# Token mean squares at a mixer's end: fifteen column products instead of row sums and transposes

## The chip, the cores and the metric

The kernel runs on one core of a Trainium2 chip. The metric is the device time of one launch in microseconds (us). The engines are TensorE (PE; its weight loads are listed apart as PEld), VectorE (DVE), ScalarE (ACT), GpSimd (POOL) and SyncE (SP), which issues most of the transfers. Each engine runs its own list of instructions in order and waits for others on semaphores.

## What is computed

A decoder trunk of two layers. Each layer adds half of a normed SwiGLU network to x, then a mixer, then half of a second SwiGLU network. All is in float32. The part that the change touches is the end of the mixer, which in the reference reads:

```python
lru_out = rmsnorm((hl * jax.nn.gelu(yl.astype(jnp.float32))).astype(h.dtype), p['lru_norm'])   # over 512 channels
...
o = rmsnorm(o, p['gla_norm']).reshape(B, T, D_GLA)                 # per head, over 128 channels, 4 heads
gla_out = (o * jax.nn.silu(g.astype(jnp.float32))).astype(h.dtype)
out = jnp.concatenate([lru_out, gla_out], axis=-1) @ p['w_out']
```

So each token needs five mean squares: one over the recurrence's 512 channels and one for each of four attention heads over its 128 channels. Each is turned into 1/sqrt(mean + eps) and multiplies that token's values.

## The kernel before

**Tiling.** The tokens are split into two groups of 288 (256 of the prompt and 32 sampled ones); channels lie on the 128 partitions, tokens along the row. There are two layers and two groups, so four mixers, numbered 0 to 3 here (mixer 1 is layer 0, group 1). A "unit" is one output tile of 128 channels: `unit` (line 446) forms it with three matmuls per input tile (the weight and the operand are each split in a high and a low part), 24 matmuls of 128x288 for a depth of 8. TensorE runs 656 units one after the other; results land in three banks of PSUM (`psD`) in turn. For each unit ScalarE makes the high part of the weight (`wh`, line 757), VectorE the low part (`wl`, line 1051, an operation with both inputs in SBUF), and VectorE or ScalarE takes the result out of its bank.

**Sides.** All else is written as generators, "sides", which each engine advances by one slot after every unit: `sides.step()`. What sets the order of the work around the change are therefore slot numbers. A mixer's attention starts after the 20 units of its input projection, and while it goes on, units of the other group's feed-forward network run. In these networks an even slot of the stretch spoken of here follows a gate unit and an odd slot an up unit. After an up unit VectorE forms `hid`, ScalarE its high part `hidh`, and GpSimd its low part `hidl` (line 1698), which waits for `hidh`. GpSimd's `sides.step()` for an odd slot comes right behind that `hidl`.

**The mixer's end.** With `T_SUMS = 31`:

- slot 2: ScalarE squares the recurrence's result into `squares` (128 x 4 x 288), long before it is needed. Slot 30: ScalarE squares the attention's result into `vT` (a part of the tile `qkv`), 4 x 288 wide, one tile per head.
- slot 31: TensorE adds the squares over the partitions with a stationary operand `pick` of 128x5, which is a column of 1/512 or 1/128 and zeros elsewhere: four matmuls of `squares` (line 687) and four of `vT` (line 690) accumulate in `psS` as 5 rows of 288. Each float32 matmul is two records in the trace. ScalarE adds eps and copies them to `rows` (line 950), with GpSimd forming the first half of `gT * oT` (line 1663) meanwhile.
- slot 32: TensorE transposes `rows` in three pieces (line 695), so that the tokens lie on 96 partitions, as 96x15. ScalarE copies that to `cols`; GpSimd's `root` raises it to -1/2 (`inv`, line 1483) and splits it in a high and a low part (`split`, lines 1491 and 1493).
- slots 34, 35 and 36: VectorE multiplies each of the five sets of 3 columns onto an identity, `diag` (line 1065, both inputs in SBUF, 96x576, two buffers), two, two and one of them; at the end of the same slots TensorE turns each into a row that is spread over all partitions (`spread`, lines 484 and 485), into `psS` for the recurrence and the four banks of `psM` for the heads. In slot 33 GpSimd forms the second half of `gT * oT` (line 1665).
- from slot 36 (`T_VALUES`): VectorE multiplies the eight tiles, ScalarE and GpSimd split them, and from unit 44 or 46 on the output projection uses them.

`columns` (line 452) is there already: for the norms between the sub-layers it takes 96 tokens' squares as the stationary operand (128x96) and a column `means` (128x1) as the moving one, so that a mean over the partitions comes out as a column of 96 partitions.

Of the kernel before, what the change touches and what calls it, by code (L numbers as in the profile page):

```python
# [12 lines left out]
P = 128  # L13
# [56 lines left out]
T_VALUES = T_SUMS + 5  # L70
# [93 lines left out]
def program(nc, a, ctx):  # L164
# [49 lines left out]
    means = sb("means", [P, 1])  # L214
    pick = sb("pick", [P, STATS, STATS])
# [40 lines left out]
    squares, val, eb, qe, gd, rows = [], [], [], [], [], []  # L256
    for g in range(G):
# [9 lines left out]
        rows.append(sb(f"rows{g}", [STATS, T]))  # L267
# [23 lines left out]
    rows_ready, rows_kept = sem("rows_ready"), sem("rows_kept")  # L291
# [135 lines left out]
    def _(e):  # L427
# [22 lines left out]
        def columns(src, first, stop):  # L450
            for t in range(NTC):
                mm = e.matmul(psS[0:TC, 0, 288 + t:289 + t], src[:, t * TC:(t + 1) * TC], means[:, :],  # L452
                              start=(first and t == 0), stop=stop, skip_group_check=True)
            return mm
# [215 lines left out]
        def attention(s):  # L670
            i, g = s.mixer, s.g
            for slot in range(T_VALUES + 2):
# [10 lines left out]
                if slot == T_SUMS:  # L683
                    sums_free()
                    e.wait_ge(lru_squared, i + 1)
                    for t in range(LT):
                        e.matmul(psS[0:STATS, 0, 0:T], pick[:, 0, :], squares[g][:, t, :], start=(t == 0), stop=False)  # L687
                    e.wait_ge(head_squared, i + 1)
                    for h in range(HEADS):
                        mm = e.matmul(psS[0:STATS, 0, 0:T], pick[:, 1 + h, :], vT[:, h, :], start=False, stop=(h == HEADS - 1))  # L690
                    mm.then_inc(rows_ready, 1)
                if slot == T_SUMS + 1:
                    e.wait_ge(rows_kept, i + 1)
                    for t in range(NTC):
                        mm = e.transpose(psS[0:TC, 0, 288 + t * STATS:288 + (t + 1) * STATS], rows[g][:, t * TC:(t + 1) * TC],
                                         ident[0:STATS, 0:STATS])
                    mm.then_inc(cols_ready, 1)
                    event[0] += 1
                    last_use.append((val_ready, 8 * i + LT))
                if slot == T_SUMS + 4:  # L700
                    spread_one()
                    e.wait_ge(s_ready, 3 * i + 3)
                for h in range(HEADS):
                    if slot == T_SUMS + 4 + (h + 1) // 2:
                        spread(psM[:, h, 0:T])
# [39 lines left out]
    def _(e):  # L745
# [182 lines left out]
        def attention(s):  # L928
            i, g = s.mixer, s.g
            for slot in range(T_VALUES + DT // 2):  # L930
# [15 lines left out]
                if slot == T_SUMS:  # L946
                    e.wait_ge(rows_ready, i + 1)
                    if i:
                        e.wait_ge(cols_kept, event[0])
                    e.activation(rows[g][:, :], psS[0:STATS, 0, 0:T], ACT.Identity, bias=epsc[0:STATS, :]).then_inc(rows_kept, 1)  # L950
                if slot == T_SUMS + 1:
                    keep_sums(STATS * NTC, True)
# [83 lines left out]
    def _(e):  # L1036
# [41 lines left out]
        def stat_diagonal(k):  # L1078
            diagonal(split[:, :, :].bitcast(F32).rearrange("p s (t k) -> p s t k", k=STATS)[:, :, :, k])
# [195 lines left out]
        def attention(s):  # L1275
            i, g = s.mixer, s.g
            for slot in range(T_VALUES + DT // 2):
# [31 lines left out]
                if slot == T_SUMS + 3:  # L1309
# [4 lines left out]
                if slot == T_SUMS + 4:  # L1314
                    stat_diagonal(2)
                    stat_diagonal(3)
                if slot == T_SUMS + 5:
# [139 lines left out]
    def _(e):  # L1457
# [184 lines left out]
        def attention(s):  # L1642
            i, g = s.mixer, s.g
            for slot in range(T_VALUES + DT // 2 + 1):
# [3 lines left out]
                for c, at in enumerate(T_QUERIES):  # L1648
# [24 lines left out]
        e.memset(means[:, :], 1.0 / D)  # L1673
        for k in range(STATS):
            e.memset(pick[:, k, k:k + 1], 1.0 / (DV if k else DL))
            if k < STATS - 1:
                e.memset(pick[:, k:k + 2, :].rearrange("p a b -> p (a b)")[:, k + 1:k + 1 + STATS], 0.0)
# [121 lines left out]
```

## Time and profile before

| what | us |
|---|---|
| median of 3 runs | 2247.0 (2244.05 to 2248.79) |
| the profiled execution, its own time | 2245.68 |
| its span in the trace | 2243.9 |
| TensorE busy | 2223.9 (99%) |
| VectorE / ScalarE / GpSimd busy | 1359.2 / 1179.7 / 734.7 |

Lines are those of the kernel before. A matmul's own duration in the rows includes its latency, and matmuls overlap: what a stretch costs TensorE is read from the distance between starts. Within a unit of the main product starts lie 0.133 us apart (24 of them take 3.2 us).

### The profile page before, as it was taken

To read this page: it belongs to the slowest core of one execution; us is meant where nothing else is said; L and a number is where in the kernel's file an instruction comes from. 1 tells how busy PE (TensorE), PEld (TensorE's weight loads), DVE (VectorE), ACT (ScalarE), POOL (GpSimd) and SP (SyncE) were. 2 spreads that over 40 slices of the span, in tenths; PEclk is the share of its full clock that TensorE was granted. 3 is DMA by queue.
4 is the path that set the end of the run, shared out by engine and by line. 5 is a ranking of instruction groups with operands and counts; after the bars stand their busy time and mean duration, and the time that the engine had idled before them with its cause. 6 is when DMAs were issued, how large, how long until landed. Compare 5 with 4: busy or idle time off the path is not lost.

```text
span 2243.9 us, 40461 instructions
## 1 busy us (share of the span) xinstructions
PE 2223.9 (99%) x16890; PEld 2187.1 (97%) x16890; DVE 1359.2 (61%) x1771; ACT 1179.7 (53%) x1840; POOL 734.7 (33%) x793
## 2 busy tenths in 40 slices
PE   9999999999999999999999999999999999999998
PEld 8999999999999999999999999999999999999998
DVE  6554757647785466755574547576578755475454
ACT  6544557536675345544454355574367653464433
POOL 4012413416544224521241124134264523252112
PEclk9999999999999999999999999999999999999999
DMA  6555555445544355555555555554354443555553
GB/s 228 161 164 165 161 169 159 132 120 163 160 147 136 117 173 155 169 160 167 162 163 165 162 167 161 167 158 129 123 176 151 142 133 122 180 161 160 166 163 129
DMA packets 102261, 350.62 MB, mean 156 GB/s; under 512 B 11296, under 2 KB 16416, under 8 KB 102080
## 3 DMA queue, kind: packets, MB, share of 16 engines
q1 hardware_dynamic: 100848, 346.76, 50.6%
q8 instruction: 135, 2.21, 0.4%
q10 hardware_dynamic: 1232, 1.27, 0.2%
q14 instruction: 46, 0.38, 0.0%
HBM read 343.12 MB, written 4.87 MB: 155 GB/s over the span
## 4 chain that ended last, share of the span: by engine, by line
PE 93%; DVE 3%; POOL 2%; issue 2%; ACT 0%; DMA 0%; SPq 0%; DVEq 0%; POOLq 0%
PE psD L446 87%; DVE wl L1051 1%; POOL ssum L1470 1%; PE psM L588 1%; DVE hl L1103 1%; PE psM L564 1%; PE psM L648 1%; PE psM L637 0%; PE psS L452 0%; DVE y L1089 0%; PE psM L666 0%; DVE x L1093 0%; PE psS L687 0%; PE psS L690 0%; DMA x<-in_xT 0%
## 5 line engine op out<-in xcount | busy, mean ns | idle before, releaser
L446 PE MATMUL psD<-hh,wh 128*128 128x288 f32 x3712 | 1111.5, 299 | 4.1 <-issue 1.3
L446 PE MATMUL psD<-hl,wh 128*128 128x288 f32 x3712 | 1098.7, 296 | 0.0
L446 PE MATMUL psD<-hh,wl 128*128 128x288 f32 x3712 | 1094.9, 295 | 0.0
L1051 DVE TENSOR_TENSOR wl<-raw,wh 128x1024 fp32r<-128x1024 f32 (+1 forms) x656 | 818.0, 1247 | 133.5 <-ACT wh L757 133.4
L757 ACT ACTIVATE wh<-raw 128x1024 fp32r<-128x1024 f32 (+1 forms) x656 | 672.4, 1027 | 106.3 <-DMA raw<-in_w_gu 52.1
L446 PEld LDWEIGHTS psD<-hh,wh 128*128 128x128 f32 x3712 | 699.3, 188 | 13.0 <-issue 8.3
L446 PEld LDWEIGHTS psD<-hh,wl 128*128 128x128 f32 x3712 | 702.5, 189 | 0.0
L446 PEld LDWEIGHTS psD<-hl,wh 128*128 128x128 f32 x3712 | 700.7, 189 | 1.0
L1698 POOL TENSOR_TENSOR hidl<-hid,hidh 128x288 fp32r<-128x288 f32 x176 | 210.0, 1193 | 941.1 <-ACT hidh L1001 941.1
L446 PE MATMUL psD<-hidh,wh 128*128 128x288 f32 x1408 | 417.5, 297 | 0.0
L446 PE MATMUL psD<-hidl,wh 128*128 128x288 f32 x1408 | 415.5, 295 | 0.0
L446 PE MATMUL psD<-hidh,wl 128*128 128x288 f32 x1408 | 415.1, 295 | 0.0
L446 PEld LDWEIGHTS psD<-hidh,wh 128*128 128x128 f32 x1408 | 264.0, 187 | 2.4 <-issue 0.7
L446 PEld LDWEIGHTS psD<-hidh,wl 128*128 128x128 f32 x1408 | 264.9, 188 | 0.0
L446 PEld LDWEIGHTS psD<-hidl,wh 128*128 128x128 f32 x1408 | 264.4, 188 | 0.0
L1470 POOL TENSOR_TENSOR ssum<-ssum,sq 128x288 f32<-128x288 f32 x166 | 193.6, 1169 | 176.7 <-ACT sq L769 173.2
L1001 ACT ACTIVATE hidh<-hid 128x288 fp32r<-128x288 f32 x176 | 78.2, 445 | 328.2 <-DVE hid L1057 328.0
L1057 DVE TENSOR_TENSOR hid<-psD,act 128x288 f32<-128x288 f32 x176 | 80.4, 457 | 258.8 <-PE psD L446 258.3
L997 ACT ACTIVATE act<-gate 128x288 f32<-128x288 f32 x176 | 78.4, 445 | 284.5 <-DVE gate L1057 283.8
L1057 DVE TENSOR_TENSOR gate<-psD,rstd 128x288 f32<-128x288 f32 x176 | 80.2, 456 | 226.8 <-PE psD L446 226.4
L1418 DVE TENSOR_TENSOR y<-psD,y 128x288 f32<-128x288 f32 x128 | 58.5, 457 | 141.0 <-PE psD L446 140.9
L1008 ACT ACTIVATE y<-psD 128x288 f32<-128x288 f32 x64 | 26.4, 413 | 119.4 <-PE psD L446 119.4
(191 smaller groups left out, 1516.2 us busy)
## 6 DMA issues: line engine op xcount, KB each, us to landing
raw<-in_w_gu SPq DMA_DIRECT2D x352, 512.0 KB, 3.6
raw<-in_w_d SPq DMA_DIRECT2D x128, 448.0 KB, 3.2
raw<-in_w_in SPq DMA_DIRECT2D x80, 512.0 KB, 3.6
raw<-in_w_d SPq DMA_DIRECT2D x64, 512.0 KB, 3.6
raw<-in_w_out SPq DMA_DIRECT2D x32, 512.0 KB, 3.6
gates<-in_w_ax SPq DMA_DIRECT2D x4, 512.0 KB, 4.7
S<-in_st_gla SPq DMA_DIRECT2D x4, 512.0 KB, 4.5
out_gla_s<-S SPq DMA_DIRECT2D x4, 512.0 KB, 5.4
```

What stands on the lines that cost most here:

```text
L446: mm = e.matmul(out, w[:, kt * P:(kt + 1) * P], t[:, kt, :], start=(kt == 0 and part == 0), stop=(kt == KT - 1 and part == 2))
L564: mm = e.matmul(psM[:, gate_of, 0:T], gates[:, t, gate_of * P:(gate_of + 1) * P], xc[g][:, :], start=True, stop=True)
L588: mm = e.matmul(psM[0:n, 2 + odd, pr * 256 + v * (n // 2):pr * 256 + (v + 1) * (n // 2)], K[rows, pr, v, 0:n], q, start=(pr == 0 and v == ...
L757: e.activation(wh[u % RING][:, 0:width], raw[u % RING][:, 0:width], ACT.Copy).then_inc(hi_ready, 1)
L997: e.activation(act[:, :], gate[:, :], ACT.Silu).then_inc(silu_ready, 1)
L1001: e.activation(hidh[:, j, :], hid[:, :], ACT.Copy).then_inc(hidh_ready, 1)
L1008: e.activation(y[g][:, m, :], bank(u), ACT.Copy).then_inc(out_taken_act, 1)
L1051: e.tensor_tensor(wl[u % RING][:, 0:width], raw[u % RING][:, 0:width], wh[u % RING][:, 0:width].bitcast(F32), ALU.subtract).then_inc(lo_re ...
L1057: e.tensor_tensor(out, bank(u), by, ALU.mult).then_inc(out_taken, 1)
L1418: e.tensor_tensor(y[g][:, m, :], bank(u), y[g][:, m, :], ALU.add).then_inc(out_taken, 1)
L1470: e.tensor_tensor(ssum[g][:, :], ssum[g][:, :], sq[g][m % 2][:, :], ALU.add).then_inc(sq_used[g], 1)
L1698: e.tensor_tensor(hidl[:, j, :], hid[:, :], hidh[:, j, :].bitcast(F32), ALU.subtract).then_inc(hidl_ready, 1)
```

## The change

The stationary operand `pick`, the tile `rows` and its two semaphores go. `means` has three columns (1/1024, 1/512 and 1/128). In slot 15 of the attention (`T_LRU_SUM`) GpSimd adds the recurrence's four tiles of squares to one, in place, in two steps. In slot 31 TensorE forms `columns` of that sum and of the four heads: 3 + 12 products with a stationary operand of 128x96 and a moving one of 128x1. The result lies in `psS` as before, but grouped by statistic, so that `stat_diagonal` takes three columns in a row. ScalarE's copy to `cols` adds eps, in slot 31, and GpSimd's `root` is in slot 31. The halves of `gT * oT` are in slots 32 and 33. The diagonals, the spreads and the values stand one slot earlier: 33 to 35, and from 35 on.

```diff
-T_VALUES = T_SUMS + 5
+T_LRU_SUM = 15
+T_VALUES = T_SUMS + 4
...
-    means = sb("means", [P, 1])
-    pick = sb("pick", [P, STATS, STATS])
+    means = sb("means", [P, 3])
...
                 if slot == T_SUMS:
                     sums_free()
-                    e.wait_ge(lru_squared, i + 1)
-                    for t in range(LT):
-                        e.matmul(psS[0:STATS, 0, 0:T], pick[:, 0, :], squares[g][:, t, :], start=(t == 0), stop=False)
+                    e.wait_ge(lru_summed, i + 1)
+                    columns(squares[g][:, 0, :], True, True, 1)
                     e.wait_ge(head_squared, i + 1)
                     for h in range(HEADS):
-                        mm = e.matmul(psS[0:STATS, 0, 0:T], pick[:, 1 + h, :], vT[:, h, :], start=False, stop=(h == HEADS - 1))
-                    mm.then_inc(rows_ready, 1)
-                if slot == T_SUMS + 1:
-                    e.wait_ge(rows_kept, i + 1)
-                    for t in range(NTC):
-                        mm = e.transpose(psS[0:TC, 0, 288 + t * STATS:288 + (t + 1) * STATS], rows[g][:, t * TC:(t + 1) * TC],
-                                         ident[0:STATS, 0:STATS])
+                        mm = columns(vT[:, h, :], False, True, 2, (1 + h) * NTC)
                     mm.then_inc(cols_ready, 1)
...
-                if slot == T_SUMS + 4:
+                if slot == T_SUMS + 3:
                     spread_one()
...
                 if slot == T_SUMS:
-                    e.wait_ge(rows_ready, i + 1)
-                    if i:
-                        e.wait_ge(cols_kept, event[0])
-                    e.activation(rows[g][:, :], psS[0:STATS, 0, 0:T], ACT.Identity, bias=epsc[0:STATS, :]).then_inc(rows_kept, 1)
-                if slot == T_SUMS + 1:
-                    keep_sums(STATS * NTC, True)
+                    keep_sums(STATS * NTC)
...
-                if slot == T_SUMS + 3:
+                if slot == T_SUMS + 2:
                     inverse_ready()
                     before = spreads[0]
                     stat_diagonal(0)
                     stat_diagonal(1)
-                if slot == T_SUMS + 4:
+                if slot == T_SUMS + 3:
...
+                if slot == T_LRU_SUM:
+                    e.wait_ge(lru_squared, i + 1)
+                    steps.mark(e.tensor_tensor(squares[g][:, 0:2, :], squares[g][:, 0:2, :], squares[g][:, 2:4, :], ALU.add))
+                    steps.after()
+                    e.tensor_tensor(squares[g][:, 0, :], squares[g][:, 0, :], squares[g][:, 1, :], ALU.add).then_inc(lru_summed, 1)
+                if slot == T_SUMS:
+                    root(STATS * NTC)
                 if slot == T_SUMS + 1:
-                    root(STATS * NTC)
-                if slot == T_SUMS:
                     e.wait_ge(g_ready, i + 1)
```

**TensorE, slot 31 of mixer 0**, between the last matmul of one unit and the first two of the next. Before:

```order
L446 MATMUL psD<-hh_53,wl_76 128x288
L687 MATMUL psS<-squares_150,pick 5x288 x4
L690 MATMUL psS<-qkv,pick 5x288 x4
L446 MATMUL psD<-hh_53,wh_59 128x288
L446 MATMUL psD<-hl_54,wh_59 128x288
```

and changed:

```order
L445 MATMUL psD<-hh_53,wl_76 128x288
L451 MATMUL psS<-means,squares_149 96x1 x3
L451 MATMUL psS<-means,qkv 96x1 x12
L445 MATMUL psD<-hh_53,wh_59 128x288
L445 MATMUL psD<-hl_54,wh_59 128x288
```

Eight float32 matmuls of 288 columns have become fifteen of one column; the three transposes that stood one unit further down are gone.

**GpSimd, slots 23 to 35 of mixer 0** (the row with x5 is the low parts of five up units, the last of them that of slot 31). Before:

```order
L1698 TENSOR_TENSOR hidl<-hid,hidh 128x288 x5
L1663 TENSOR_TENSOR gT<-gT,oT 128x576
L1483 TENSOR_TENSOR inv<-cols,minus_half 96x15
L1491 CAST split<-inv 96x15
L1493 TENSOR_TENSOR split<-inv,split 96x15
L1698 TENSOR_TENSOR hidl<-hid,hidh 128x288
L1665 TENSOR_TENSOR gT<-gT,oT 128x576
L1698 TENSOR_TENSOR hidl<-hid,hidh 128x288
```

and changed (the last three places of the list are the low part of slot 33's unit, the second half of `gT * oT`, and the low part of slot 35's):

```order
L1687 TENSOR_TENSOR hidl<-hid,hidh 128x288 x5
L1470 TENSOR_TENSOR inv<-cols,minus_half 96x15
L1478 CAST split<-inv 96x15
L1480 TENSOR_TENSOR split<-inv,split 96x15
L1655 TENSOR_TENSOR gT<-gT,oT 128x576
L1687 TENSOR_TENSOR hidl<-hid,hidh 128x288
L1657 TENSOR_TENSOR gT<-gT,oT 128x576
L1687 TENSOR_TENSOR hidl<-hid,hidh 128x288
```

The root has moved ahead of the low part of slot 33's unit. The second `gT` is right behind that low part in both, but what VectorE has to do at that time is another thing now, as the next lists show.

**VectorE, slots 33 to 35 of mixer 0** (`hid` and `gate` take a unit's result out of its bank). Before:

```order
L1057 TENSOR_TENSOR hid<-psD,act 128x288
L1051 TENSOR_TENSOR wl_75<-raw_69,wh_63 128x896
L1057 TENSOR_TENSOR gate<-psD,rstd_81 128x288
L1051 TENSOR_TENSOR wl_76<-raw_70,wh_64 128x896
L1065 TENSOR_TENSOR diag_89<-ident,split 96x576
L1065 TENSOR_TENSOR diag_88<-ident,split 96x576
L1057 TENSOR_TENSOR hid<-psD,act 128x288
L1051 TENSOR_TENSOR wl_71<-raw_65,wh_59 128x896
L1065 TENSOR_TENSOR diag_89<-ident,split 96x576
L1065 TENSOR_TENSOR diag_88<-ident,split 96x576
```

and changed:

```order
L1044 TENSOR_TENSOR hid<-psD,act 128x288
L1038 TENSOR_TENSOR wl_75<-raw_69,wh_63 128x896
L1052 TENSOR_TENSOR diag_89<-ident,split 96x576
L1052 TENSOR_TENSOR diag_88<-ident,split 96x576
L1044 TENSOR_TENSOR gate<-psD,rstd_81 128x288
L1038 TENSOR_TENSOR wl_76<-raw_70,wh_64 128x896
L1052 TENSOR_TENSOR diag_89<-ident,split 96x576
L1052 TENSOR_TENSOR diag_88<-ident,split 96x576
L1044 TENSOR_TENSOR hid<-psD,act 128x288
L1038 TENSOR_TENSOR wl_71<-raw_65,wh_59 128x896
```

The first two diagonals stood behind a `gate` (an even slot), in which GpSimd has no low part to form; now they stand behind a `hid` (an odd slot).

## Rows read from the trace of the kernel before

**Rows 1.** The page's first part: busy time, share of span, instructions of each engine.

```profile
PE 2223.9 (99%) x16890; PEld 2187.1 (97%) x16890; DVE 1359.2 (61%) x1771; ACT 1179.7 (53%) x1840; POOL 734.7 (33%) x793
```

**Rows 2.** Timeline of TensorE, mixer 0's sums: start us, us, line, names, count.

```profile
496.75 0.29 PE L446 MATMUL psD<-hh,wl 128*128 128x288 f32 x1
496.97 2.10 PE L687 MATMUL psS<-squares,pick 128*5 128x288 f32 x8
...
501.18 0.30 PE L446 MATMUL psD<-hl,wh 128*128 128x288 f32 x1
...
504.11 0.29 PE L446 MATMUL psD<-hh,wl 128*128 128x288 f32 x1
...
504.81 0.29 PE L446 MATMUL psD<-hl,wh 128*128 128x288 f32 x1
```

**Rows 3.** Timeline of TensorE at two places where column products stand already.

```profile
640.93 0.29 PE L446 MATMUL psD<-hh,wl 128*128 128x288 f32 x1
641.07 0.59 PE L452 MATMUL psS<-means,ssum 128*96 128x1 f32 x6
641.52 0.38 PE L446 MATMUL psD<-hh,wh 128*128 128x288 f32 x1
641.73 0.29 PE L446 MATMUL psD<-hl,wh 128*128 128x288 f32 x1
...
2024.52 0.29 PE L446 MATMUL psD<-hh,wl 128*128 128x288 f32 x1
...
2025.84 0.30 PE L446 MATMUL psD<-hl,wh 128*128 128x288 f32 x1
```

**Rows 4.** Timeline of TensorE around the first two spreads, mixers 0 and 3.

```profile
514.14 0.29 PE L446 MATMUL psD<-hh,wl 128*128 128x288 f32 x1
...
514.90 0.30 PE L446 MATMUL psD<-hidh,wh 128*128 128x288 f32 x1
...
1892.90 0.29 PE L446 MATMUL psD<-hh,wl 128*128 128x288 f32 x1
...
1894.28 0.29 PE L446 MATMUL psD<-hh,wh 128*128 128x288 f32 x1
```

**Rows 5.** Timeline of VectorE at the spreads of mixer 0, then mixer 3.

```profile
513.00 1.41 DVE L1065 TENSOR_TENSOR diag<-ident,split 96x576 fp32r<-96x576 f32 x2
514.57 0.46 DVE L1057 TENSOR_TENSOR hid<-psD,act 128x288 f32<-128x288 f32 x1 [0.16 <-PE psD L446]
514.94 1.08 DVE L1051 TENSOR_TENSOR wl<-raw,wh 128x896 fp32r<-128x896 f32 x1
515.94 2.03 DVE L1065 TENSOR_TENSOR diag<-ident,split 96x576 fp32r<-96x576 f32 x2
...
1890.40 2.05 DVE L1051 TENSOR_TENSOR wl<-raw,wh 128x1024 fp32r<-128x1024 f32 x1
```

**Rows 6.** Timeline of GpSimd at the same two places.

```profile
515.59 1.11 POOL L1698 TENSOR_TENSOR hidl<-hid,hidh 128x288 fp32r<-128x288 f32 x1 [3.46 <-ACT hidh L1001]
...
1889.95 1.43 POOL L1665 TENSOR_TENSOR gT<-gT,oT 128x576 f32<-128x576 f32 x1
```

**Rows 7.** Timelines of GpSimd, VectorE and TensorE in mixer 0's slots 14 to 16.

```profile
428.87 4.54 POOL L1630 TENSOR_TENSOR qf<-dec,qkv 128x768 f32<-128x768 f32 x2
...
431.61 2.75 DVE L1236 TENSOR_TENSOR kf<-dec,qkv 128x896 f32<-128x896 f32 x1
...
436.04 0.38 PE L617 MATMUL psM<-ident,kf 128*128 128x128 f32 x2
```

**Rows 8.** Busy time (count) by stretch: PE, PEld, DVE, ACT, POOL; PEclk, DMA share, GB/s.

```profile
482.00:483.00 1.00, 1.00 (x12) 0.98 (x12) 0.00 (x0) 0.00 (x0) 0.00 (x0) 0.50 0.33 123
486.00:489.00 3.00, 3.00 (x15) 3.00 (x14) 0.00 (x0) 0.00 (x0) 0.00 (x0) 0.54 0.00 0
757.00:762.00 5.00, 5.00 (x22) 5.00 (x23) 0.00 (x0) 0.00 (x0) 0.00 (x0) 0.52 0.00 0
628.00:629.00 1.00, 0.14 (x1) 0.15 (x1) 1.00 (x3) 0.98 (x3) 0.67 (x2) 0.85 0.78 315
```

More of the change, by code:

```diff
@@ L255, in program @@
     xc, rg, ig, tau, aa, l1, l2 = ([], [], [], [], [], [], [])
-    squares, val, eb, qe, gd, rows = [], [], [], [], [], []
+    squares, val, eb, qe, gd = [], [], [], [], []
     for g in range(G):
@@ L266, in program @@
         qe.append(sb(f"qe{g}", [P, PR, C]))
-        rows.append(sb(f"rows{g}", [STATS, T]))
         assert cursor[0] <= result_at[g] + DT * T * 4
@@ L290, in program @@
     setup_v, setup_a, setup_p, wgdh_ready, wgdl_ready = (sem(k) for k in ("setup_v", "setup_a", "setup_p", "wgdh_ready", "wgdl_ready"))
-    rows_ready, rows_kept = sem("rows_ready"), sem("rows_kept")
+    lru_summed = sem("lru_summed")
     sq_ready, sq_used = [sem(f"sq_ready{g}") for g in range(G)], [sem(f"sq_used{g}") for g in range(G)]
@@ L448, in unit, with columns @@
             mm.then_inc(unit_done, 1)
-        def columns(src, first, stop):
+        def columns(src, first, stop, k=0, at=0):
             for t in range(NTC):
-                mm = e.matmul(psS[0:TC, 0, 288 + t:289 + t], src[:, t * TC:(t + 1) * TC], means[:, :],
+                mm = e.matmul(psS[0:TC, 0, 288 + at + t:289 + at + t], src[:, t * TC:(t + 1) * TC], means[:, k:k + 1],
                               start=(first and t == 0), stop=stop, skip_group_check=True)
@@ L703, in attention @@
                 for h in range(HEADS):
-                    if slot == T_SUMS + 4 + (h + 1) // 2:
+                    if slot == T_SUMS + 3 + (h + 1) // 2:
                         spread(psM[:, h, 0:T])
@@ L1078, in stat_diagonal @@
         def stat_diagonal(k):
-            diagonal(split[:, :, :].bitcast(F32).rearrange("p s (t k) -> p s t k", k=STATS)[:, :, :, k])
+            diagonal(split[:, :, k * NTC:(k + 1) * NTC].bitcast(F32))
         def inverse_ready():
@@ L1313, in attention @@
                     stat_diagonal(1)
-                if slot == T_SUMS + 4:
+                if slot == T_SUMS + 3:
                     stat_diagonal(2)
                     stat_diagonal(3)
-                if slot == T_SUMS + 5:
+                if slot == T_SUMS + 4:
                     stat_diagonal(4)
@@ L1672, in _ @@
         e.memset(ones[:, :].bitcast(F32), 1.0)
[L1673 to L1677, printed above, removed]
+        for k, width in enumerate((D, DL, DV)):
+            e.memset(means[:, k:k + 1], 1.0 / width)
         e.memset(qkvs[:, 0:PR], DK ** -0.5)
```

## Prediction

> **What bounds the kernel now.** I read the busy times first, and there is little to choose: TensorE is busy for 2223.9 of 2243.9 us, 99%, the others for 61% or less [rows 1]. A microsecond of work less on TensorE is a microsecond less of time, as long as nobody makes it wait in return; and a wait anywhere else costs nothing until TensorE has it. So the views to read are the timelines of TensorE at the mixers' ends, and then those of the two engines that must have the diagonals ready for it. The reader should look at distances between starts there, not at durations: two neighbouring matmuls of a unit start 0.133 us apart, and whatever stands between them costs the distance less 0.133 us for each ordinary step.
>
> **What goes from TensorE.** In mixer 0 the last matmul of a unit starts at 496.75, the row sums at 496.97, and the second matmul of the next unit at 501.18 [rows 2]. That is 4.43 us with two ordinary steps in it, so the eight float32 matmuls cost 4.43 - 0.27 = 4.16 us. The transposes: from 504.11 to 504.81 [rows 2], 0.70 - 0.27 = 0.43 us. Together 4.59 us a mixer, and the other three mixers have the same distances within 0.02 us.
>
> **What comes to TensorE.** Column products stand in the trace already, with the same 128x96 operand and the same moving column. Three of them (six records) lie between 640.93 and 641.73: 0.80 - 0.27 = 0.53 us. Six, in two groups with a wait between that is long fulfilled, lie between 2024.52 and 2025.84: 1.32 - 0.27 = 1.05 us [rows 3]. So three cost 0.53 us and each further three 0.52, and fifteen cost 0.53 + 4 x 0.52 = 2.61 us. The ends: 2.25 us, if all went like the first three, which take 0.45 us from their first start at 641.07 to 641.52, and 2.65 us, if each three paid the 0.53. The gain is 4.59 - 2.61 = 1.98 us a mixer, 7.9 us in all (7.8 to 9.4).
>
> What these products spend is the load of their stationary operand, a fresh one for each record: 0.52 us for six loads is 87 ns each. The Trainium skill, page "TensorE: Matmul & The Clock Gate", section "LDWEIGHTS (loading the stationary operand)", gives a load as its columns over 1.2, which is an estimate of 80 ns for 96 columns and 2.4 us for the thirty. By that page the gain would be 8.8 us rather than 7.9; the rows of this trace decide, and they say 87.
>
> **The sum of squares on GpSimd** is a 128x576 and a 128x288 operation. The nearest rows are a 128x576 product, 1.43 us, and a low part of 128x288, 1.11 us [rows 6], so 2.5 us a mixer. In slot 15 of mixer 0 it comes behind the two `qf` that end at 433.41, while VectorE's `kf`, started at 431.61, is waiting [rows 7]; `kf` gets its turn first (below) and ends at 434.36 as before, and TensorE needs it only at 436.04, 1.7 us later. Should GpSimd's first addition get ahead of `kf`, it would still be there in time. Everything behind it on GpSimd (the exponents of the third chunk, `qe`) moves by 2.5 us and has several slots. I take nothing; the upper end is the 0.8 us by which both additions together, ahead of `kf`, would overrun the 1.7, in the two mixers of group 0.
>
> **The diagonals** are where I see the gain go. Rows 5 and 6 show a rule of this kernel: a VectorE operation with both inputs in SBUF and a GpSimd operation do not run at the same time, and they take turns. Two diagonals take 1.41 us when GpSimd is idle and 2.03 us when the low part `hidl` (from 515.59) is waiting: `hidl` gets the gap between `wl` and the first diagonal. In mixer 3 `wl`, which for its 1024 columns would take some 1.2 us by the 1.08 for 896, takes 2.05 because the second half of `gT * oT` runs from 1889.95 for 1.43 us [rows 5, 6]. The Trainium skill says the same on its page "SBUF — State Buffer", section "Who interferes with whom": an exclusive lock that is held for a whole instruction, not a split of the bandwidth. By that rule, which these rows bear out, the turns below follow.
>
> Before, the first two diagonals stood behind a gate unit, the next two behind an up unit. Now the first two stand behind the up unit of slot 33, and GpSimd has two operations for that moment, `hidl` and right behind it the second `gT`. I lay the old slot 35 under the new slot 33: its unit's last matmul starts at 514.14 [rows 4], `hid` 514.57, `wl` 514.94 to 516.02, `hidl` waits from 515.59 and ends at 516.70, the first diagonal is done at about 517.33 and the second at 517.97 [rows 5, 6]. With `gT` queued behind `hidl`, `gT` gets the turn after the first diagonal and holds it for 1.3 us, and the second diagonal ends at 519.3. TensorE, one gate unit of 3.2 us further on, arrives at the first spread at 514.14 + 3.2 + 0.13 = 517.47, finds it ready, and at the second at 517.74, where it waits until 519.35: 1.6 us. Then `hid`, `gate` and the later diagonals catch up, since the next pair stands behind a gate unit with an idle GpSimd.
>
> Before, the same pair cost in mixer 0 (514.14 to 514.90, less one step and four spread matmuls of 0.133) 0.10 us of waiting, in mixer 3 (1892.90 to 1894.28) 0.71 [rows 4]; mixers 1 and 2, read alike, 0.36 and 0.10, in all 1.3 us. Now it is 4 x 1.6 = 6.4 us, so 5.1 us more. The fifth diagonal, behind an up unit too, may bring 0.3 us in the mixers of group 0, and the later pair no longer waits 0.3: nothing, in sum. The ends for the diagonals: 0 (the turns fall otherwise) and 7 us.
>
> **TensorE's clock.** The trace shows that the clock falls from 2.4 to 1.2 GHz (granted 1.00 to 0.50) not only when TensorE idles, as between 628 and 629 us, where it is busy for 0.14 us, but also while it is 100% busy with matmuls of few columns: at 482 us of mixer 0, behind the sampled tokens' outputs, it stands at 0.50 [rows 8]. Fifteen products of one column for 2.6 us are such a stretch; the row sums streamed 288 columns each, and the clock stayed up. A fall costs what the full products behind it lose. In 486 to 489 us there are 15 matmuls where 22.5 would start: 1.0 us lost; in 757 to 762, 22 for 37.5: 2.1 us lost [rows 8]. Those stretches behind the outputs are longer (4.9 to 6.8 us) than 2.6, and the column products of before, at most 1.05 us at once, never brought a fall. 2.6 us lies between, so the price is 0 to 2.1 us a mixer, and I take 1.5 us in one or two of the four: 2.2 us. It is nearest to the idle stretch at 628 us.
>
> **The sum.** -7.9 + 5.1 + 2.2 = -0.6 us. The profiled execution took 2245.68 us, its span and 1.8 us around it; the median of the runs is 1.3 us above it, and the sum is small enough to carry over: 2246.4 us.
>
> **The rivals.** (a) The turns fall otherwise and the diagonals come in time. For it speaks that GpSimd's operations could reach their turn earlier than I laid them, or `gT` a little before `hidl`; against it that the two stand side by side in the program and the old slot 35 shows each step. Then the gain stays: 2247.0 - 7.9 = 2239.1 us without a fall of the clock, 2241.3 with the falls taken above. (b) Slower: the clock falls at every mixer's end and at the dearer price. -7.9 + 5.1 + 4 x 2.1 = +5.6, 2252.6 us. It decides from two falls at the dearer price on, with the waits as worked out: below that the kernel is no slower than before. For it speaks that one column in 87 ns is almost nothing to do; against it that 2.6 us is short. (c) Waits as forecast and no fall at all: -2.8 us, 2244.2. (d) The change doesn't reach the time, because the products do not run at the pace of rows 3: if the 2.6 us became the old 4.6, only the waits would be left, 2252.1.
>
> **How the numbers follow.** Waits at the diagonals and up to three falls of the clock, 2244 to 2249, with 2246.4 in the middle: 0.57 (with rival c in it, 0.2). Rival a: 0.26. Rival b: 0.12. Rival d and what I don't see: 0.05. A measurement of this kernel can tell about 0.2%, 4.5 us, from no change; that is 2242.5 to 2251.5. Nearly all of rival a is faster by more, nearly all of b and d slower by more. So faster 0.27, same 0.59, slower 0.14. The range reaches into rival a down to 2240 and to 2251.5 above; outside are the deepest part of a and most of b and d, 2 in 10.
>
> **What would show it.** In the changed profile: 4.43 us between the starts around slot 31 should be 2.9; no transposes. Between the first and the second spread of each mixer TensorE should wait 1.6 us for VectorE's `diag`, with `hidl` and `gT` of GpSimd in between the two diagonals, which as a pair should take 3.3 us. If they take 1.4 to 2.0, rival a holds. The granted clock behind slot 31 should be 0.5 in one or two of the four mixers. VectorE's `kf` of slot 15 should end where it did. I am wrong if the wait is missing, or if the sum of squares on GpSimd turns up as a wait of TensorE.

## The result, and the profile after

The changed kernel takes 2249.6 us (median of 20 runs, 2246.35 to 2252.53), against 2245.5 us (20 runs, 2243.73 to 2248.79) for the kernel before on the same chip. The ratio is 1.0018, interval 1.0012 to 1.0024: 4.1 us slower, where 2246.4 had been forecast, 0.6 below the median then known. The time lies inside the range, but the small gain has become a small loss. The profiled executions say the same: the span went from 2243.9 to 2247.8 us.

The first part of the profile's page after: busy time, share of the span, instructions.

```profile
PE 2221.9 (99%) x16934; PEld 2197.0 (98%) x16934; DVE 1365.0 (61%) x1771; ACT 1178.0 (52%) x1836; POOL 753.3 (34%) x794
```

TensorE is busy for 2.0 us less than in [rows 1], in a span that is 3.9 us longer: it waits more, and its busy time did not get shorter by the 7.9 us expected. VectorE is busy 5.8 us longer: its diagonals take 7.4 us more (30.1 to 37.5), its `wl` 1.7 us less.

**The products.** Timeline of TensorE in slot 31 of mixer 0, the place of [rows 2] (start, duration, engine, line, names, count):

```profile
495.08 0.29 PE L445 MATMUL psD<-hh,wl 128*128 128x288 f32 x1
495.21 0.59 PE L451 MATMUL psS<-means,squares 128*96 128x1 f32 x6
495.67 2.18 PE L451 MATMUL psS<-means,qkv 128*96 128x1 f32 x24
497.71 0.39 PE L445 MATMUL psD<-hh,wh 128*128 128x288 f32 x1
497.92 0.41 PE L445 MATMUL psD<-hl,wh 128*128 128x288 f32 x1
```

From 495.08 to 497.92 are 2.84 us, less two ordinary steps of 0.13: 2.57 us for the fifteen products, where 2.61 were forecast. The transposes are gone.

**The diagonals.** Timelines of VectorE and GpSimd, and then of TensorE at the first two spreads, mixer 0; what stands in brackets is idle time before an instruction, and what ended it:

```profile
506.38 1.08 DVE L1038 TENSOR_TENSOR wl<-raw,wh 128x896 fp32r<-128x896 f32 x1
507.38 3.24 DVE L1052 TENSOR_TENSOR diag<-ident,split 96x576 fp32r<-96x576 f32 x2
...
507.02 1.10 POOL L1687 TENSOR_TENSOR hidl<-hid,hidh 128x288 fp32r<-128x288 f32 x1 [4.11 <-ACT hidh L988]
508.09 1.92 POOL L1657 TENSOR_TENSOR gT<-gT,oT 128x576 f32<-128x576 f32 x1
...
508.77 0.29 PE L445 MATMUL psD<-hh,wl 128*128 128x288 f32 x1
...
510.76 0.37 PE L483 MATMUL psM<-diag,ones 96*128 96x288 f32 x1 [1.44 <-DVE diag L1052]
...
511.11 0.29 PE L445 MATMUL psD<-hh,wh 128*128 128x288 f32 x1
```

Two diagonals take 3.24 us, with `hidl` and `gT * oT` of GpSimd taking turns with them; beside an idle GpSimd they took 1.41, and beside `hidl` alone 2.03 [rows 5]. The rule of the Trainium skill, page "SBUF — State Buffer", section "Who interferes with whom" (an exclusive lock for a whole instruction), is borne out: with the second `gT` queued too, the pair is 1.21 us longer than beside `hidl` alone, and an undisturbed `gT * oT` takes 1.41 us in this kernel. From 508.77 to 511.11, less one step and four spread matmuls (0.67), TensorE loses 1.67 us. The other mixers, read alike: 1.82, 1.69 and 2.17. Mixer 3 loses more because TensorE waits before its first spread too:

```profile
1891.03 0.40 PE L483 MATMUL psS<-diag,ones 96*128 96x288 f32 x1 [0.22 <-DVE diag L1052]
...
1892.99 0.37 PE L483 MATMUL psM<-diag,ones 96*128 96x288 f32 x1 [1.43 <-DVE diag L1052]
```

**The clock.** Busy time in five stretches of the changed kernel (TensorE, its loads, VectorE, ScalarE, GpSimd, each with its count; then TensorE's granted clock, the DMA share and GB/s). The first four lie behind slot 31 of the four mixers, the fifth behind the spreads of mixer 3:

```profile
498.00:501.00 3.00, 3.00 (x14) 3.00 (x13) 0.00 (x0) 0.15 (x1) 2.75 (x1) 0.50 0.02 6
768.00:771.00 3.00, 3.00 (x15) 3.00 (x14) 0.00 (x0) 0.00 (x0) 2.85 (x3) 0.50 0.04 12
1608.00:1610.00 2.00, 2.00 (x10) 2.00 (x10) 0.00 (x0) 0.00 (x0) 1.94 (x1) 0.50 0.00 0
1881.00:1883.00 2.00, 2.00 (x11) 2.00 (x10) 0.00 (x0) 0.00 (x0) 1.93 (x2) 0.50 0.00 0
1894.00:1897.00 3.00, 3.00 (x15) 3.00 (x14) 1.69 (x3) 0.54 (x1) 0.00 (x0) 0.50 0.03 5
```

All four mixers lose the clock right behind the products, with TensorE 100% busy; 14 or 15 matmuls start in 3 us instead of 22.5. The kernel before has none of these; its own falls [rows 8] stand elsewhere. The fifth fall is another matter: it begins at 1894.0, less than a microsecond behind the waits of mixer 3, and not behind the products.

**The account.** Every distance between two starts of TensorE, less 0.133 us for an ordinary step, sorted by what stands between. A main step is one between two matmuls of units:

| us beyond ordinary steps, whole kernel | before | after | change |
|---|---|---|---|
| sums of squares and transposes, with the step back into the unit | 18.4 | 10.3 | -8.1 |
| spreads and waits for diagonals | 11.6 | 17.3 | +5.7 |
| main steps at a granted clock of 0.50 | 9.3 | 16.1 | +6.9 |
| work behind the sampled tokens' outputs | 22.3 | 21.4 | -0.9 |
| idle at starts of layers, and the rest | | | +0.3 |
| sum | | | +3.9 |

Against the terms of the forecast, -7.9, +5.1 and +2.2, the third is the one that failed: 6.9 us in place of 2.2.

### The profile page after: what moved, and what is told of

It is laid out like the page before. It is cut to its first block, busy times and chain, and to the rows that moved or that the text cites. A ratio compares the mean times of both kernels' runs of the same rounds, so it can differ in the third digit from the quotient of the medians.

```text
span 2247.8 us, 40543 instructions
## 1 busy us (share of the span) xinstructions
PE 2221.9 (99%) x16934; PEld 2197.0 (98%) x16934; DVE 1365.0 (61%) x1771; ACT 1178.0 (52%) x1836; POOL 753.3 (34%) x794
## 4 chain that ended last, share of the span: by engine, by line
PE 92%; DVE 4%; POOL 2%; issue 2%; ACT 0%; DMA 0%; SPq 0%; DVEq 0%; POOLq 0%
PE psD L445 86%; DVE wl L1038 1%; PE psS L451 1%; POOL ssum L1457 1%; PE psM L587 1%; DVE hl L1090 1%; PE psM L563 1%; PE psM L647 1%; DVE diag L1052 1%; PE psM L636 0%; DVE y L1076 0%; PE psM L665 0%; DVE x L1080 0%; DMA x<-in_xT 0%; PE psM L593 0%
## 5 line engine op out<-in xcount | busy, mean ns | idle before, releaser
L1090 DVE SCALAR_TENSOR_TENSOR hl<-x,par,hh 128x288 fp32r<-128x288 f32 x96 | 88.7, 934 | 0.7 <-ACT hh L782 0.7
```

The source lines that it names most:

```text
L1090: e.scalar_tensor_tensor(hl[g][:, m, :], x[g][:, m, :], col(par, l * NPAR + PRE + st * DT + m), hh[g][:, m, :].bitcast(F32), ALU.mult, ALU ...
```

## The experiments

In the expectations, T is the theory that the thin products themselves bring the clock down; R1, that the wait at the diagonals does (the fifth fall above stands right behind such a wait); R2, that GpSimd's sum of squares costs time. "Block" is all fifteen products in one slot. Each ratio is against runs of the kernel before on the same chip, whose medians were 2245.75, 2246.07 and 2245.6 us on the three chips used; intervals are 95%. Each trace shows one execution of its kernel.

### The wait away, the block kept

```diff
-                if slot == T_SUMS + 2:
                     e.tensor_tensor(gT[:, 2:4, :], gT[:, 2:4, :], oT[:, 2:4, :], ALU.mult).then_inc(og_ready, 1)
```

The second half of `gT * oT` stands right behind the first, a slot before the diagonals.

> The changed kernel with one edit: the second half of gT * oT stands right behind the first, in slot 32, and no longer behind the low part of slot 33's unit. Theory T (two costs, each its own: the turns that VectorE and GpSimd take at the first two diagonals, and falls of TensorE's clock brought by the fifteen column products themselves): the pair of diagonals takes 2.0 us instead of 3.24, TensorE's wait between the first two spreads goes from 1.7 to about 0.3 us, and the time falls by 4 x 1.4 = 5.5 us to about 2244; the clock still falls behind slot 31 in all or nearly all mixers. Rival R1 (the clock falls because TensorE waits at the diagonals): the falls behind slot 31 go too, and the time comes to about 2238. Rival R2 (the cost is GpSimd's sum of squares or something else): less than 2 us from the changed kernel.

2245.18 us (11 runs), ratio 0.9998 (0.9990 to 1.0007): 4.4 us less than the changed kernel. Timelines of VectorE and GpSimd, mixer 0, and the clock behind slot 31 in mixers 0 and 1:

```profile
509.18 2.03 DVE L1052 TENSOR_TENSOR diag<-ident,split 96x576 fp32r<-96x576 f32 x2
...
508.82 1.11 POOL L1686 TENSOR_TENSOR hidl<-hid,hidh 128x288 fp32r<-128x288 f32 x1 [2.68 <-ACT hidh L988]
...
500.00:503.00 3.00, 3.00 (x14) 3.00 (x13) 0.00 (x0) 0.00 (x0) 2.89 (x2) 0.50 0.00 0
770.00:772.00 2.00, 2.00 (x10) 2.00 (x10) 0.00 (x0) 0.01 (x1) 1.92 (x1) 0.50 0.12 49
```

The pair is back at 2.03 us and the waits shrink to 0.47, 0.60, 0.47 and 0.95 us (0.3 had been expected), so 4.9 of 7.4 us of waiting go by the traces, and 4.4 us by the medians where 5.5 had been expected. All four falls behind the products stay: R1 is out for these. The fifth, behind the spreads of mixer 3, is gone together with most of the wait there.

### The block away

Three, six and six products, a unit between them, instead of fifteen.

```diff
-T_SUMS = 31
+T_SUMS = 32
...
-                if slot == T_SUMS:
+                if slot == T_SUMS - 2:
                     sums_free()
                     e.wait_ge(lru_summed, i + 1)
                     columns(squares[g][:, 0, :], True, True, 1)
+                if slot == T_SUMS - 1:
                     e.wait_ge(head_squared, i + 1)
-                    for h in range(HEADS):
+                    for h in (0, 1):
+                        columns(vT[:, h, :], False, True, 2, (1 + h) * NTC)
+                if slot == T_SUMS:
+                    for h in (2, 3):
                         mm = columns(vT[:, h, :], False, True, 2, (1 + h) * NTC)
...
-                if slot == T_SUMS - 1:
+                if slot == T_SUMS - 2:
                     e.wait_ge(o_kept, 3 * i + 3)
```

The halves of `gT * oT` are in slots 31 and 33, around the diagonals of slot 34.

> The changed kernel with the fifteen products in three places: the recurrence's three in slot 30, six for heads 0 and 1 in slot 31, six for heads 2 and 3 in slot 32; the root, both halves of gT * oT, the diagonals and the spreads stand in the slots that they have in the kernel before. T: no block is longer than 1.05 us, so the clock doesn't fall more often than in the kernel before, the waits at the diagonals are those of before, and the gain of the products is left: 8.1 us less two further re-entries of 0.09 us in each mixer, 7.4 us, so 2238. R1 says the same here. R2 (GpSimd's sum costs what was lost): 2241 or more.

2239.0 us (5 runs), ratio 0.9967 (0.9955 to 0.9980); the same kernel again, on another chip:

> The version in three places (2239.0 in five runs) once more, on the same chip as its variants: 1 us above the one with the early gT.

2236.17 us (5 runs, 2234.2 to 2242.1), ratio 0.9962 (0.9950 to 0.9974). The stretches from ahead of the products to behind the first spreads, mixers 0 and 3, first of the two profiles:

```profile
493.00:508.00 15.00, 15.00 (x125) 15.00 (x125) 8.34 (x10) 6.58 (x10) 6.69 (x6) 1.00 0.41 123
...
1865.00:1882.00 17.00, 17.00 (x140) 17.00 (x139) 9.25 (x12) 7.67 (x12) 8.88 (x7) 1.00 0.41 122
```

The granted clock is 1.00 throughout, in mixers 1 and 2 and in the second profile also. In these two executions the same fifteen products, dealt over three slots, bring no fall. Both profiles are of the quicker executions of this version, 2236.03 and 2234.2 us; the slower ones are spoken of under the next experiment.

### The block away, the wait kept

The same three places a slot later (`T_SUMS = 33`: slots 31, 32 and 33), with the halves of `gT * oT` at the distances that they have in the changed kernel.

> As the version in three places, but everything one slot later and with the changed kernel's distances: products in slots 31, 32 and 33, the diagonals from slot 35 (behind an up unit) with the second half of gT * oT behind the low part of slot 35. So the wait at the diagonals is there and the long block isn't. T: TensorE waits about 1.7 us (2.1 in the mixers of group 0, where the unit between is 0.4 us shorter) at the second spread, no fall of the clock behind the products: 2238 + 5.7 + 0.8 = about 2244.5. R1: the falls stay, about 6 us more, 2250.

2245.22 us (11 runs), ratio 0.9997 (0.9988 to 1.0007). VectorE's and GpSimd's timelines, TensorE's at the second spread, and two stretches of mixer 0, from the last products on and around the wait:

```profile
512.34 3.25 DVE L1056 TENSOR_TENSOR diag<-ident,split 96x576 fp32r<-96x576 f32 x2
...
513.05 1.92 POOL L1661 TENSOR_TENSOR gT<-gT,oT 128x576 f32<-128x576 f32 x1
...
515.73 0.38 PE L483 MATMUL psM<-diag,ones 96*128 96x288 f32 x1 [1.45 <-DVE diag L1056]
...
503.00:506.00 3.00, 3.00 (x28) 3.00 (x28) 1.46 (x2) 1.44 (x3) 1.46 (x2) 1.00 0.48 137
510.00:517.00 7.00, 5.55 (x39) 5.02 (x38) 6.04 (x7) 2.31 (x5) 3.85 (x3) 1.00 0.43 140
```

The wait is back in full (3.25 us for the pair, 1.45 us of idle TensorE; over the four spread matmuls 1.90, 1.68, 1.89 and 1.67 us are lost in the four mixers), and the clock stays up through products and waits in all four mixers.

That is so in the execution that was profiled, which took 2242.14 us, the third fastest of eleven. The granted clock averaged over a whole execution is 0.994 in it, 0.995 in the fastest (2240.63 us), 0.991 at the median and 0.989 in the slowest (2251.31 us). The version in three places does the same: 0.994 at 2236.03 us, 0.991 at 2242.28, and 0.991 at 2242.06 on the other chip. The changed kernel has 0.989 to 0.991 in all of its executions. So the slower executions of these versions had more falls than the profiled ones, and no trace shows where. The traces show that products in three places need not bring the clock down; they do not show that the products, or the waits, never do.

The four kernels make a square:

| median, us | fifteen in one slot | in three slots |
|---|---|---|
| `gT * oT` between the diagonals | 2249.6 | 2245.2 |
| out of their way | 2245.2 | 2239.0 and 2236.2 |

The block costs 4.4 us in the upper row and 6.2 to 9.0 in the lower one, the wait 4.4 in the left column and 6.2 to 9.0 in the right. Two steps of about 4.4 would lead to 2240.8; the lower right corner lies below that. Part of it is that the corner has one more difference: its first diagonals stand in slot 34, behind a gate unit, where GpSimd has no low part to form. The waits at the spreads are 7.3 and 2.5 us in the left column and 7.1 and 1.4 in the right one, so 1.1 us of the lower row are not the block's. The other part is the falls in the slower executions. The profiled executions alone are 2249.6 and 2245.2 us on the left and 2242.1 and 2236.0 (2234.2 again) on the right: by them the block costs 7.5 us in the upper row, near the five falls that are gone, 5 x 1.5 us.

### How many in one slot

First, as in the kernel with the wait away, but with the recurrence's three products moved to slot 29, so that twelve remain:

```diff
-                if slot == T_SUMS:
+                if slot == T_SUMS - 2:
                     sums_free()
                     e.wait_ge(lru_summed, i + 1)
                     columns(squares[g][:, 0, :], True, True, 1)
+                if slot == T_SUMS:
                     e.wait_ge(head_squared, i + 1)
```

> The version with the early second half of gT * oT, and of the fifteen products the recurrence's three in slot 29; twelve stay in slot 31. T: the block is 2.1 us instead of 2.6, so the clock should fall less often than in all four mixers: between 2239.0 (no fall more than before) and 2244 (as with fifteen in one block). If the falls had nothing to do with the block's length, 2244.

2242.27 us (11 runs), ratio 0.9982 (0.9973 to 0.9990), 2.9 us below fifteen at once. Stretches behind slot 31 of mixers 0, 1 and 3:

```profile
500.00:503.00 3.00, 3.00 (x16) 3.00 (x15) 0.00 (x0) 0.00 (x0) 2.93 (x2) 0.56 0.06 22
770.00:773.00 3.00, 3.00 (x15) 3.00 (x14) 0.00 (x0) 0.00 (x0) 2.90 (x3) 0.50 0.17 66
...
1876.00:1880.00 4.00, 4.00 (x33) 4.00 (x32) 0.36 (x2) 0.59 (x2) 3.82 (x4) 1.00 0.26 98
```

With 2.1 us of products at once, three of the four mixers fall in this execution. The fourth gets back less than a fall costs: TensorE comes sooner to the spreads there and waits 1.45 us in place of 0.95. Then, from the version with three places and early `gT * oT` (below), nine products in slot 31 and six in slot 32, an edit of the same kind:

> The version in three places with the early gT, but in two places: nine products (1.57 us) in slot 31 and six in slot 32. T (falls of the clock come with the length of the thin stretch: none behind 1.05 us, three of four mixers behind 2.1, all four behind 2.6): no or few falls behind 1.6 us, one re-entry of 0.09 us fewer in each mixer, so within 2 us of the version in three places. If nine in a row bring the clock down in most mixers: 4 to 6 us above it.

2235.01 us (6 runs), ratio 0.9955 (0.9942 to 0.9967). Mixer 0's stretch reads:

```profile
493.00:508.00 15.00, 15.00 (x125) 15.00 (x124) 8.16 (x10) 6.58 (x10) 8.24 (x7) 1.00 0.39 122
```

No mixer falls behind 1.6 us of products at once in this execution; the other three read 1.00 as well. And the other way, the recurrence's four tiles of squares each with products of their own, no sum on GpSimd, 24 products in slot 31:

```diff
-                    e.wait_ge(lru_summed, i + 1)
-                    columns(squares[g][:, 0, :], True, True, 1)
+                    e.wait_ge(lru_squared, i + 1)
+                    for n in range(LT):
+                        columns(squares[g][:, n, :], n == 0, n == LT - 1, 1)
```

> The version with the early second half of gT * oT (2245.2), without GpSimd's additions: TensorE forms the recurrence's sum by twelve products instead of three, 24 in a row in slot 31. Nine more products at 0.174 us are 1.57 us a mixer, 6.3 us: 2251.5 with the falls of the clock as they are (one in each mixer behind the sums). If a longer block brings longer falls (two stretches instead of one), up to 6 us more, 2257.

2255.59 us (4 runs), ratio 1.0047 (1.0034 to 1.0061), 10.4 us above the kernel with fifteen. TensorE in mixer 0, and two stretches there:

```profile
495.65 2.12 PE L451 MATMUL psS<-means,squares 128*96 128x1 f32 x24
497.63 3.83 PE L451 MATMUL psS<-means,qkv 128*96 128x1 f32 x24
501.32 0.59 PE L445 MATMUL psD<-hh,wh 128*128 128x288 f32 x1
...
498.00:501.00 3.00, 3.00 (x20) 3.00 (x21) 0.00 (x0) 0.00 (x0) 0.19 (x1) 0.50 0.15 61
501.00:504.00 3.00, 3.00 (x14) 3.00 (x15) 0.00 (x0) 0.27 (x1) 2.16 (x1) 0.50 0.00 0
```

The clock falls inside the block: the first 24 records start within 1.98 us, 83 ns each, the next 24 within 3.69, 154 ns each. Nine products more would be 4 x 1.57 = 6.3 us at full clock; in the traces the four blocks grow by 9.7 us, so 3.5 us are products slowed by the falls. In mixers 0, 2 and 3 the falls also last longer than with fifteen products. The page "TensorE: Matmul & The Clock Gate" of the Trainium skill, section "LDWEIGHTS (loading the stationary operand)", gives a load by its columns alone, an estimate of 80 ns for these, and names no clock beside it; at the full clock the trace comes near that, with 83 ns, and at half clock, with 154 ns, it does not.

### Wide work between the products

Fifteen products in slot 31 as in the kernel with the wait away, with a matmul of 288 columns, whose result nothing uses, behind each of the first four groups of three:

```diff
+                    wide(T)
                     e.wait_ge(head_squared, i + 1)
                     for h in range(HEADS):
                         mm = columns(vT[:, h, :], False, True, 2, (1 + h) * NTC)
+                        if h < HEADS - 1:
+                            wide(T)
```

> The version with the early second half of gT * oT (2245.2) with all fifteen products in slot 31, and four matmuls of 128x288 in between, one behind each three products, whose results nobody reads. T (the clock falls because so little streams through TensorE for 2.6 us): the four of them cost 0.15 to 0.25 us each, 2.4 to 4 us in all, and the falls behind slot 31 go, 6 us less: 2242 to 2244, faster with more work. Rival (the falls come from something else in slot 31, the float32 loads or the place in the program): 2248 to 2249.

2247.72 us (11 runs), ratio 1.0007 (0.9998 to 1.0016): 2.5 us more, which is what the four matmuls take (0.6 us a mixer). TensorE at the first groups of mixer 1, and the clock behind slot 31 in mixers 0 and 1:

```profile
769.41 0.59 PE L451 MATMUL psS<-means,squares 128*96 128x1 f32 x6
769.86 0.38 PE L456 MATMUL psS<-wgp,ones 128*128 128x288 f32 x1
770.08 0.59 PE L451 MATMUL psS<-means,qkv 128*96 128x1 f32 x6
...
500.00:503.00 3.00, 3.00 (x16) 3.00 (x16) 0.00 (x0) 0.27 (x1) 1.59 (x1) 0.50 0.05 18
503.00:506.00 3.00, 3.00 (x14) 3.00 (x14) 0.00 (x0) 0.00 (x0) 2.86 (x4) 0.50 0.00 0
773.00:776.00 3.00, 3.00 (x15) 3.00 (x14) 0.00 (x0) 0.00 (x0) 2.87 (x2) 0.50 0.02 5
```

All four falls stay, and those of mixers 0 and 2 last longer than with the plain block (the second row above is still at 0.50; there the products had ended by 500.9). One wide matmul between groups of three does not prevent what a whole unit between groups of six does. T as I had put it missed here: a break of wide work in the products was to keep the clock up, and one of this size does not. The rival's forecast, 2248 to 2249, was the nearer one. What is left of T is that the block of products brings the fall, and that it did not come where a unit's worth of wide work stood between small groups. The place in the program is out as a cause, since slot 31 holds six or nine products in versions without these falls. Whether it is the few columns or the many loads of a stationary operand that matter was not separated by any run: both went together in all of them.

### Both costs away, and the sum of squares

Three places as above, both halves of `gT * oT` in slot 31, ahead of everything:

```diff
-                if slot == T_SUMS + 1:
                     e.tensor_tensor(gT[:, 2:4, :], gT[:, 2:4, :], oT[:, 2:4, :], ALU.mult).then_inc(og_ready, 1)
```

> The version in three places (2239.0) with both halves of gT * oT in slot 31. T: GpSimd has nothing left at the first two diagonals, so TensorE's wait there (0.12 to 0.45 us over the four spread matmuls, 1.1 us in the four mixers) goes: 2238. If turns of VectorE and GpSimd had nothing to do with it, 2239 as before the edit.

2233.73 us (5 runs), ratio 0.9947 (0.9933 to 0.9961). And again on another chip:

> The version in three places with both halves of gT * oT in slot 31 once more, beside the same without that edit on the same chip. By the waits in the traces (1.1 us over the four mixers without the edit, none at the first pair with it) it should be 1 us faster than the version in three places; the 5.3 us between their first medians would then be the spread of few runs.

2233.56 us (5 runs, 2233.3 to 2236.6), ratio 0.9949 (0.9937 to 0.9961). VectorE's diagonals of mixer 0 and the stretch of its sums, second of the two:

```profile
510.53 1.42 DVE L1056 TENSOR_TENSOR diag<-ident,split 96x576 fp32r<-96x576 f32 x2
...
493.00:508.00 15.00, 15.00 (x125) 15.00 (x124) 8.63 (x10) 6.58 (x10) 8.13 (x7) 1.00 0.40 123
```

The first pair has GpSimd idle beside it: 1.42 us, as in [rows 5], and TensorE does not wait for it (only the later pair costs 0.3 us of waiting in mixers 0 and 2). No fall behind the products. This is the fastest version, 12.0 us (0.5%) below the kernel before and 16 below the changed one. Both forecasts were too cautious: 2238 us had been expected, and 1 us below the version in three places on the same chip, where 2.6 were measured. The waits at the spreads account for 0.8 us of that; the rest goes with the clock, 0.994 at this version's median and 0.993 at the other's.

Two kernels without GpSimd's additions, a copy of one element in their place (their recurrence's mean is therefore that of one tile of four); first with `gT * oT` in slots 31 and 33, then with both halves early:

```diff
-                    steps.mark(e.tensor_tensor(squares[g][:, 0:2, :], squares[g][:, 0:2, :], squares[g][:, 2:4, :], ALU.add))
-                    steps.after()
-                    e.tensor_tensor(squares[g][:, 0, :], squares[g][:, 0, :], squares[g][:, 1, :], ALU.add).then_inc(lru_summed, 1)
+                    e.tensor_copy(tail[:, 0, 0:1], tail[:, 0, 0:1]).then_inc(lru_summed, 1)
```

> The version in three places without GpSimd's two additions in slot 15: a copy of one element takes their place in the order, so the recurrence's mean is that of one tile of four only; the outputs depend on it, the work of the rest doesn't. My step that the additions cost nothing: 2239, within 1 us of the version with them. Rival R2 (they hold VectorE up and so TensorE): 1.5 us or more less, up to 2.5 us in each mixer, 2229.

> The same version without GpSimd's two additions in slot 15 (a copy of one element in their place, so the recurrence's mean is that of one tile of four). My step that the additions cost TensorE nothing: the same as with them within 1 us. Rival R2: 1.5 us or more below.

2236.14 us (5 runs) with ratio 0.9959 (0.9946 to 0.9971), beside 2236.17 and 2239.0 with the sum; 2233.43 us (5 runs) with ratio 0.9945 (0.9933 to 0.9957), beside 2233.56 and 2233.73 with it. The last pair ran on one chip and its executions lie close together (four of five within 0.3 us in one, all but one within 0.1 in the other), so it can tell: the sum of squares costs 0.1 us or nothing. R2 is out.

## Why the prediction was wrong, point by point

**What bounds the kernel**: right. The 3.9 us between the two traces are found on TensorE's own list.

**The products**: right. 2.57 us measured for the 2.61 worked out from [rows 3]; with the step back into the unit -8.1 us over the four mixers for -7.9. Rival d, that they run no faster than the sums before, did not come.

**The sum of squares on GpSimd**: right, and shown by the two kernels without it. In mixer 0 it lies where [rows 7] put it:

```profile
433.31 2.28 POOL L1647 TENSOR_TENSOR squares<-squares 128x576 f32<-128x576 f32 x1
435.67 1.55 POOL L1649 TENSOR_TENSOR squares<-squares 128x288 f32<-128x288 f32 x1
...
431.55 2.75 DVE L1223 TENSOR_TENSOR kf<-dec,qkv 128x896 f32<-128x896 f32 x1
```

Alone it would be 2.5 us; it takes 3.9. The first addition waits its turn behind `kf`, which ends at 434.30, as before; the second takes turns with VectorE's next `wl`, which takes 1.44 us in place of 1.08. TensorE waits for neither.

**The diagonals**: mechanism and turns as forecast, 3.24 us for 3.3, in this order. The waits came to 1.67, 1.82, 1.69 and 2.17 us, 7.4 in all where 4 x 1.6 = 6.4 stood; mixer 3 carries half of the miss, since there TensorE waits before the first spread too. Net +5.7 for +5.1. Rival a, the turns otherwise, did not come.

**The clock**: the step that failed. "I take 1.5 us in one or two of the four: 2.2 us." The price of one fall was right: the half-pace steps behind the four blocks of products cost 1.52 us each, and those behind the spreads of mixer 3 the same, together 7.6 us; the falls elsewhere came to 0.7 less than before, net 6.9. The number of falls was not: all four mixers fell, and mixer 3 a second time behind its spreads, which no term of the forecast had. The prediction had seen that 2.6 us of thin products lie between 1.05, which never brought a fall, and 4.9, which did; it settled near the lower end and had no reason for it. The profiled executions have since filled the gap: no fall behind 0.53, 1.05 or 1.6 us at once, three of four behind 2.1, four of four behind 2.6, and four of four with the 24 products (4.1 us at full clock), in three of them before the block had ended. A place between two bounds on an effect that either comes or doesn't should have weighed "in all four" beside "in none", since the four mixers run the same program; "one or two of four" was a mean over those cases, not the likeliest of them. Rival b had the mechanism but asked 2.1 us a fall for it; with 4 x 1.5 it would have given -7.9 + 5.1 + 6.0 = +3.2, near the +3.9 of the traces. That the time still lay inside the range is owed to the range's width, not to the middle of it.

**The sum.** -8.1 + 5.7 + 6.9 - 0.6 = +3.9 between the profiled executions, +4.1 between the medians. A gain of 8 us was real, and 12.6 us were given back on the same engine, 5.7 by an unlucky order on GpSimd and 6.9 by the clock; with both repaired the kernel is 12 us faster than before.

**What stays open.** The second profile of the fastest version is 12.1 us shorter than that of the kernel before. By the distances between starts the sums give 8.0 of it, the waits at the spreads 1.1, and main steps at half clock 3.0 (6.3 us in place of 9.3). Those last falls stand where the kernel before has them too, behind the sampled tokens' outputs and where TensorE idles between layers, near 628 and 1738 us. Whether such a fall comes differs behind the same idling: TensorE idles for 2.15 us before 628.86 in the kernel before, and the clock falls; it idles for 2.14 us before 628.06 in the changed one, and the granted clock stays at 1.00. What decides was not found. Nor is it known where the slower executions of the versions in three places have their further falls. The versions whose TensorE waits at the first diagonals spread more (2240.6 to 2251.3 us with the waits in full, 2234.2 to 2242.3 with 1.4 us of them) than those without that wait in three places (2232.3 to 2236.8), so the waits may have a part in it, as R1 had it and as the fifth fall suggests. That is argued, not shown, and one execution with nine and six products and no such wait took 2241.34 us. The times of one kernel also bunch about 1.5 us apart (changed kernel: 2246.35, 2248.1, 2249.5, 2251.1, 2252.5), which fits one fall more or less each and agrees with the clock going down as the time goes up; that too is argued. How much wide work between the products is enough was not tried.

## What to carry to other kernels

Replacing wide matmuls with a block of thin ones saves TensorE's time and can lose it again through the clock: put the thin ones in small groups with whole units of wide work between, and look at the granted clock behind each group. Before a VectorE operation with both inputs in SBUF that TensorE waits for, keep GpSimd's queue empty: an operation that isn't urgent there belongs a slot earlier. And when the same program runs in several places, "in all of them" is a case with a chance and a price of its own, beside "in none"; a mean over the two is not the likeliest outcome.

## What the runs showed of the hardware that I had not expected

A TensorE that is 100% busy can lose its clock: behind 2.6 us of one-column products, 87 ns each record, it went from 2.4 to 1.2 GHz in four mixers of four, and four matmuls of 288 columns among them did not keep it up. An idle TensorE can keep it: the granted clock stayed at 1.00 through four idle stretches of about 1.45 us in the profiled execution of the kernel with the wait kept, and through one of 2.14 us near 628 in the changed kernel. The Trainium skill, page "TensorE: Matmul & The Clock Gate", section "HAM oscillation — how this bites in real kernels", names waits for data between bursts as what brings the clock down. The fall behind 2.15 us of idling at 628 in the kernel before fits that; those behind the products do not, and there the trace decides.

A fall that comes while thin products are still under way slows these too: they went from 83 to 154 ns a record.
